# Adding the feed-forward output panels to the residual by ScalarE copies and an accumulating transfer

## What is computed

```python
def swiglu(hn, w_in, w_out):
    gate, up = jnp.split(jnp.einsum('btd,de->bte', hn, w_in), 2, axis=-1)
    return jnp.einsum('btf,fd->btd', jax.nn.silu(gate) * up, w_out)
...
        h = h + swiglu(rmsnorm(h, ffn_norm[i]), ffn_w_in[i], ffn_w_out[i])
        gate = jax.nn.sigmoid(jnp.einsum('btd,de->bte', rmsnorm(h, ple_norm[i]), ple_w_gate[i]))
        h = h + gate * jnp.einsum('btk,kd->btd', p[i], ple_w_proj[i])
    return rmsnorm(h, final_norm)
```

## Time and profile before

| | us |
|---|---|
| median of 3 runs (1648.51 to 1648.92) | 1648.61 |
| the profiled execution's own time | 1648.48 |
| span of its instructions | 1646.7 |
| TensorE busy | 1628.0 |
| VectorE busy | 1224.7 |
| ScalarE busy | 853.0 |

### The profile page before, as it was taken

The page is one execution under the profiler, slowest core; times in us unless marked ns, Lnnn a source line. Parts: engine busy times, 40 slices in busy tenths (PEclk is TensorE's granted clock), DMA queues, the critical chain, the costliest instruction groups (busy, mean ns, idle before and its releaser), DMA issues.

```text
span 1646.7 us, 21708 instructions
## 1 busy us (share of the span) xinstructions
PE 1628.0 (99%) x8508; PEld 1340.5 (81%) x8508; DVE 1224.7 (74%) x1168; ACT 853.0 (52%) x880; POOL 58.6 (4%) x83
## 2 busy tenths in 40 slices
PE   9999999999999999999998999999999999999997
PEld 7888888888888888888887888888888888887886
DVE  5544475566787999765588988988888888888654
ACT  5444454443567655765464545454555544554543
POOL 7000000000010000000000000000000000000001
PEclk9999999999999999999999999999999999999999
DMA  8666655766575655545565546456457366365741
GB/s 277 179 181 189 185 161 167 230 220 215 155 256 166 180 178 180 167 132 181 176 227 205 184 174 243 165 204 229 146 212 254 121 235 238 119 237 215 289 153 51
DMA packets 156776, 316.00 MB, mean 192 GB/s; under 512 B 7360, under 2 KB 7360, under 8 KB 155808
## 3 DMA queue, kind: packets, MB, share of 16 engines
q1 hardware_dynamic: 155088, 304.12, 56.7%
q0 software_dynamic: 1616, 10.87, 1.8%
HBM read 310.77 MB, written 4.19 MB: 191 GB/s over the span
## 4 chain that ended last, share of the span: by engine, by line
PE 97%; DVE 1%; issue 1%; ACT 1%; DMA 0%; POOLq 0%; POOL 0%; DVEq 0%; SPq 0%; ACTq 0%
PE acc L732 15%; PE acc L734 15%; PE acc L733 15%; PE acc L1031 9%; PE acc L1033 9%; PE acc L1032 9%; PE aux L1031 7%; PE aux L1033 7%; PE aux L1032 7%; PE aux L748 1%; PE aux L918 1%; DVE d_lo L2136 1%; PE aux L760 1%; PE acc L1059 0%; PE aux L812 0%
## 5 line engine op out<-in xcount | busy, mean ns | idle before, releaser
L2136 DVE TENSOR_TENSOR d_lo<-d_raw,d_hi 128x2048 fp32r<-128x2048 f32 x181 | 414.1, 2289 | 120.9 <-ACT d_hi L1492 88.8
L1668 DVE TENSOR_TENSOR w_lo<-w_raw,w_hi 128x1024 fp32r<-128x1024 f32 x276 | 335.9, 1224 | 207.6 <-ACT w_hi L1191 207.0
L1191 ACT CAST w_hi<-w_raw 128x1024 fp32r<-128x1024 f32 x276 | 289.5, 1050 | 341.5 <-PE acc L734 312.7
L1492 ACT CAST d_hi<-d_raw 128x2048 fp32r<-128x2048 f32 x137 | 262.3, 1915 | 234.4 <-PE acc L1033 128.9
L732 PE MATMUL acc<-w_hi,a_hi 128*128 128x512 f32 x832 | 330.8, 398 | 0.0
L733 PE MATMUL acc<-w_lo,a_hi 128*128 128x512 f32 x832 | 324.6, 390 | 0.0
L734 PE MATMUL acc<-w_hi,a_lo 128*128 128x512 f32 x832 | 324.6, 390 | 0.0
L734 PEld LDWEIGHTS acc<-w_hi,a_lo 128*128 128x128 f32 x832 | 156.2, 188 | 33.1
L732 PEld LDWEIGHTS acc<-w_hi,a_hi 128*128 128x128 f32 x832 | 156.3, 188 | 31.9 <-issue 0.3
L733 PEld LDWEIGHTS acc<-w_lo,a_hi 128*128 128x128 f32 x832 | 156.5, 188 | 30.6
L1504 ACT CAST d_hi<-d_raw 128x2048 fp32r<-128x2048 f32 x44 | 84.2, 1913 | 124.0 <-PE aux L1033 66.8
(11 more groups left out here) (312 smaller groups left out, 2218.0 us busy)
## 6 DMA issues: line engine op xcount, KB each, us to landing
d_raw<-in_ffn_w_in SPq DMA_DIRECT2D x88, 1024.0 KB, 7.4
w_raw<-in_w_in SPq DMA_DIRECT2D x112, 512.0 KB, 3.7
w_raw<-in_gla_w_in SPq DMA_DIRECT2D x96, 512.0 KB, 3.9
d_raw<-in_ffn_w_out SPq DMA_DIRECT2D x44, 1024.0 KB, 5.1
w_raw<-in_w_out SPq DMA_DIRECT2D x32, 512.0 KB, 4.7
w_raw<-in_gla_w_out SPq DMA_DIRECT2D x32, 512.0 KB, 3.7
d_raw<-in_ple_w_gate SPq DMA_DIRECT2D x16, 1024.0 KB, 5.1
x_raw<-in_x_cols SPq DMA_DIRECT2D x8, 256.0 KB, 7.0
```

What stands on the lines that cost most here:

```text
L1191: nc.scalar.copy(w_hi[u % RING][:], w_raw[u % RING][:]).then_inc(hi_done, 1)
L1492: nc.scalar.copy(d_hi[e % SPLITS][:], d_raw[slot][:]).then_inc(d_hi_done, 1)
L1668: nc.vector.tensor_tensor(w_lo[u % RING][:], w_raw[u % RING][:], w_hi[u % RING][:], ALU.subtract).then_inc(lo_done, 1)
L2136: nc.vector.tensor_tensor(d_lo[e % SPLITS][:], d_raw[slot][:], d_hi[e % SPLITS][:], ALU.subtract).then_inc(d_lo_done, 1)
```

## The change

VectorE no longer adds o0 to o3 to the residual, in any of the ten steps. ScalarE copies each of the 40 panels (80 banks) into one of two buffers `out_copy`, of 512 KB each, in SBUF that the kernel no longer needs by then, and raises `out_read`. POOL waits for each copied panel and issues an accumulating transfer from the buffer to `h_tok` in SBUF, which raises `out_added`. ScalarE waits for `out_added` of the panel two before, before it fills a buffer again. The adds of fe0 to fe3 stay on VectorE (`add_last`), which now also waits until all 20 transfers of the buffer for even or odd panels have landed. POOL issues `emb_back` and `fin_w` from inside this sequence, behind the transfer of o1 of the last step.

```diff
+    out_copy = [at(f"out_copy{r}", [P, TT, N], F32, (48 + 4 * r) * KB) for r in range(2)]
...  # gpsimd
+            def load_last():
                 pool.wait_ge(d_used, LAST["ft4"] + 1)
                 pool.wait_ge(act_ready, TT * NF)
                 pool.wait_ge(emb_out, 16)
                 pool.dma_start(emb_back[:], emb_dram).then_inc(emb_in, 16)
                 pool.dma_start(fin_w[:], final_norm.partition_broadcast(P)).then_inc(fin_in, 16)
+            for m in range(PO * (NF - 1)):
+                pool.wait_ge(out_read, TT * (m + 1))
+                pool.dma_start(h_tok[:, :, (m % PO) * N:(m % PO + 1) * N], out_copy[m % 2][:],
+                               accum_op=ALU.add).then_inc(out_added[m % 2], 16)
+                if m == PO * (NF - 1) - 3:
+                    load_last()
...  # tensor: turn_h2 and the fe panels
-                pe.wait_ge(out_read, tiles_before + TT * (n + 1))
+                pe.wait_ge(fe_read, TT * (n + 1))
...  # scalar
+            def copy_out(n, e, f, i=0, banks=acc[0:2], first=False):
+                act.wait_ge(d_used, i * E_STEP + (e + 1))
+                if n >= 2 or not first:
+                    act.wait_ge(out_added[n % 2], i * 32 + (32 * (f - 1) + 16 * (n // 2)))
+                for t, b in enumerate(banks):
+                    nc.scalar.copy(out_copy[n % 2][:, t, :], b[:]).then_inc(out_read, 1)
                 silu(1, f - 1, i)
+                if not first:
+                    copy_out(3, before["o3"], f - 1, i)
                 quad_high(at, "g1", f, i)
...
                 quad_high(at, "u1", f, i)
+                copy_out(0, at["o0"], f, i, first=first)
                 sum_high(at, "ft2", f, i)
                 if not last:
                     quad_high(at, "o1", f, i)
                     sum_high(at, "ft3", f, i)
                     quad_high(at, "o2", f, i)
                     silu(0, f, i)
+                    copy_out(1, at["o1"], f, i, first=first)
                     sum_high(at, "ft4", f, i)
                     quad_high(at, "o3", f, i)
+                    copy_out(2, at["o2"], f, i)
                 else:
...
                     quad_high(at, "o3", f, i)
+                    copy_out(1, at["o1"], f, banks=acc[2:4])
...
             high_of(E_FE, ("fe", 0))
+            copy_out(2, LAST["o2"], NF - 1)
             split_act(NF - 1, last_hi, aux[0:2])
+            high_of(E_FE + 1, ("fe", 1))
+            copy_out(3, LAST["o3"], NF - 1, banks=acc[2:4])
...  # vector: add_out leaves all its places in ffn_step and behind fe_low(0) and fe_low(1)
-            def add_out(n, e, i=0, banks=acc[0:2]):
-                dve.wait_ge(d_used, i * E_STEP + (e + 1))
+            def add_last(n):
+                dve.wait_ge(d_used, E_FE + n + 1)
+                dve.wait_ge(out_added[n % 2], 32 * (NF - 1))
                 s = slice(n * N, (n + 1) * N)
-                for t, b in enumerate(banks):
-                    nc.vector.tensor_tensor(h_tok[:, t, s], h_tok[:, t, s], b[:], ALU.add).then_inc(out_read, 1)
+                for t, b in enumerate(panel_banks(n)):
+                    nc.vector.tensor_tensor(h_tok[:, t, s], h_tok[:, t, s], b[:], ALU.add).then_inc(fe_read, 1)
```

More of the change, by code:

```diff
@@ L464, in block_kernel @@
         act_turned, act_hi_done, act_lo_done = (sem(n) for n in ("act_turned", "act_hi_done", "act_lo_done"))
-        out_read, gate_read = sem("out_read"), sem("gate_read")
+        out_read, fe_read, gate_read = sem("out_read"), sem("fe_read"), sem("gate_read")
+        out_added = [sem(f"out_added{r}") for r in range(2)]
         block = ctx.enter_context(nc.Block())
@@ L697, in _ @@
             nc.gpsimd.tensor_tensor(rstd[2][:], ms[:], minus_half[:], ALU.pow).then_inc(rstd_done, 1)
[L699 to L703, removed]
+            def load_last():
+                pool.wait_ge(d_used, LAST["ft4"] + 1)
+                pool.wait_ge(act_ready, TT * NF)
+                pool.wait_ge(emb_out, 16)
+                pool.dma_start(emb_back[:], emb_dram).then_inc(emb_in, 16)
+                pool.dma_start(fin_w[:], final_norm.partition_broadcast(P)).then_inc(fin_in, 16)
+            for m in range(PO * (NF - 1)):
[4 more added lines that the diff above has]
+                    load_last()
             pool.wait_ge(fin_in, 16)
@@ L1152, in _ @@
             for n in range(PO):
-                pe.wait_ge(out_read, tiles_before + TT * (n - 1))
+                if n < 2:
+                    pe.wait_ge(out_read, tiles_before + TT * (n - 1))
+                else:
+                    pe.wait_ge(fe_read, TT * (n - 1))
                 quad(E_FE + n, late_banks(n), last_hi, last_lo, 0, True, BOTH)
@@ L1159, in _ @@
                 if n < 2:
-                    pe.wait_ge(out_read, tiles_before + TT * (n + 3))
+                    pe.wait_ge(fe_read, TT * (n + 3))
                 else:
@@ L1577, in split_act, with ffn_step @@
                     nc.scalar.copy(token_half(dst[:, 0:N // P, :], k), by_half(banks[k][:])).then_inc(act_hi_done, 1)
-            def ffn_step(at, f, i=0, last=False):
+            def copy_out(n, e, f, i=0, banks=acc[0:2], first=False):
[4 more added lines that the diff above has]
+                    nc.scalar.copy(out_copy[n % 2][:, t, :], b[:]).then_inc(out_read, 1)
+            def ffn_step(at, before, f, i=0, first=False, last=False):
                 quad_high(at, "g0", f, i)
@@ L1608, in ffn_step @@
                     quad_high(at, "o3", f, i)
-            ffn_step(STEP, 1)
+                    copy_out(1, at["o1"], f, banks=acc[2:4])
+            ffn_step(STEP, FIRST, 1, first=True)
+            before = {name: e - E_STEP for name, e in STEP.items()}
             with act.Fori(1, NF - 2) as i:
-                ffn_step(STEP, 1, i)
-            ffn_step(LAST, NF - 1, last=True)
+                ffn_step(STEP, before, 1, i)
+            ffn_step(LAST, items(NF - 2), NF - 1, last=True)
             high_of(E_FE, ("fe", 0))
+            copy_out(2, LAST["o2"], NF - 1)
             split_act(NF - 1, last_hi, aux[0:2])
-            for n in range(1, PO):
+            high_of(E_FE + 1, ("fe", 1))
+            copy_out(3, LAST["o3"], NF - 1, banks=acc[2:4])
+            for n in range(2, PO):
                 high_of(E_FE + n, ("fe", n))
@@ L2278, in ffn_step @@
                     combine_first_up()
-                else:
-                    add_out(3, before["o3"], i)
                 quad_low(at, "g1", f, i)
@@ L2292, in ffn_step @@
                 quad_low(at, "u1", f, i)
-                add_out(0, at["o0"], i)
                 quad_low(at, "ft2", f, i)
@@ L2300, in ffn_step @@
                     quad_low(at, "o2", f, i)
-                    add_out(1, at["o1"], i)
                     quad_low(at, "ft4", f, i)
@@ L2304, in ffn_step @@
                     quad_low(at, "o3", f, i)
-                    add_out(2, at["o2"], i)
                     multiply(0, f, i)
@@ L2317, in ffn_step @@
                     quad_low(at, "o3", f)
-                    add_out(1, at["o1"], banks=acc[2:4])
             ffn_step(STEP, FIRST, 1, first=True)
@@ L2330, in _ @@
             fe_low(0)
-            add_out(2, LAST["o2"])
             split_act(NF - 1, last_hi, last_lo, aux[0:2])
             fe_low(1)
-            add_out(3, LAST["o3"], banks=acc[2:4])
             fe_low(2)
             fe_low(3)
-            add_out(0, E_FE, banks=late_banks(0))
+            add_last(0)
             for n in range(PO - 1):
                 low_of(E_PG + n, RAW[("pg", n)][0])
-                add_out(n + 1, E_FE + n + 1, banks=late_banks(n + 1))
+                add_last(n + 1)
                 split_h("h2", n, V_PLE)
```

## The result

The changed kernel takes 1668.93 us in the median of 4 runs (1666.57 to 1670.61), the kernel before 1648.56. The ratio is 1.0122, with a 95% interval from 1.0109 to 1.0135: 20 us slower, where 7.5 were forecast. The profiled execution is the longest of the four, 1670.61 us with a span of 1668.9; what follows explains its 22.2 us of span over the 1646.7 of before.

A forecast was written before the change was run, and what follows sets the result against it. TensorE, busy 99% of the span, was taken to bound the kernel. 1648.5 + 0 (adds) + 0 (copies) + 4.5 (loop) + 3.3 (end) = 1656.3, and 0.1 for the median: 1656 us; range 1648 to 1672.

The forecast's parts named there:

- The wait for `cx`: Last step: TensorE's 2.3 us wait for a VectorE combine stays despite the removed adds; gain 0.
- I take 2.4: Engine time chosen for one accumulating transfer, 2.4 us, nearer the upper end of 1.35 to 2.7.
- A: Time one 512 KB accumulating transfer holds the 16 DMA engines; taken as 2.4 us, range 1.35 to 2.7.
- a room of 3.1 us: Step boundary: g1's tile may land 3.1 us after 1202.32, at 1205.3, before TensorE has to wait.
- the formula: Step boundary: two accumulations ahead make g1 land 2A - 0.45 us later; 4.5 us over nine boundaries.
- two-item leads: Loop: casts of ft4, o3 and g0 come 1.1 us later behind ScalarE's copies, hidden inside these leads.
- The end, 3.3 forecast: Last step: 1.6 us of wait ahead of the first transposes plus 1.7 for the clock, 3.3 us.
- 1529.2 + A: Last step: fe3's tile, landing at 1529.2 before, now lands at 1531.6, giving 1.6 us of wait.
- The second mechanism of the text: Last step: o2's transfer, queued behind 3 MB of loads, lands at 1535; `add_last(0)` wants it at 1534.19; 1 us.
- The hidden case: Rival, no change: each transfer costs near 1.35 us and stays hidden, 1649; chance 0.40 together with ScalarE's 2 us at most.
- The slow adder: Rival: at 4 us a transfer, g1 lands 3.0 to 4.5 us late at nine boundaries, 1704; chance 0.13.
- ScalarE's room of 0.9 us ahead of o1: Loop: the copy of o0 delays o1's subtraction by 1.1 us, leaving 0.9 of 2.0 us of room; hidden.

The follow-up runs named there:

- the copies alone: Changed kernel with ScalarE's 80 copies but no transfers and no waits for them, so o0 to o3 are not added: 1649.00 us, ratio 1.0003.
- The plain transfer: Changed kernel with the 40 transfers overwriting the residual instead of adding to it: 1652.38 us, ratio 1.0025.
- o1 and o2 alone: Changed kernel with only the transfers of o1 and o2 issued (20 of 40), o0 and o3 copied and not added: 1664.74 us, ratio 1.0101.
- only o0 and o3: Changed kernel with only the transfers of o0 and o3 issued (20 of 40), o1 and o2 copied and not added: 1649.12 us, ratio 1.0002.
- four buffers: Changed kernel with four copy buffers, o1 to o3 transferred after the load burst except in the last step, two last loads behind all transfers: 1648.25 us, ratio 0.9997.
- the last loads behind: Changed kernel with the two loads of 3 MB issued behind all 40 transfers, not behind the 38th: 1664.68 us, ratio 1.0095.

## Why the prediction was wrong

**Direction and places: right.** Slower, by two things, and both are where the text had them: nine waits of TensorE at g1, because the engines serve two accumulations before its load is through, and one ahead of the first transposes, because fe3's tile comes late beside what POOL issues. The removed adds and the added copies were put at 0 and are 0 (the copies alone, 1.0003). The wait for `cx` was to stay and stayed. The sum was wrong: 7.8 us against 22.1 in the profiled execution. The range held the measured time, the terms did not hold theirs.

**The step that failed is "I take 2.4" for A.** It measured 2.8. The price of a wait at g1 is what is left of a room of 3.1 us, so a small error of A is a large one of the wait. With A = 2.8 and the rest of the text's own working, g1 would land 2 x 2.8 - 0.45 = 5.15 us later, which is 0.6 to 2.1 us late, about 1.3 on the mean and 12 for nine. Measured: 12.6. In the text 0.5 on the mean and 4.5. The bounds were wrong too: the upper one, both operands read at the rate of a plain move, was 2.7. The plain transfer has A = 1.3, against the 1.35 of the lower bound, so the adding one costs 2.2 times a plain one. The rule of the Trainium skill (Collectives: The Full Stack, section "The bandwidth ceiling: the fold count and why AG ≠ RS ≠ AR"), half the bandwidth for a reducing transfer, agrees with the runs better than my choice did: 2.8 against 1.3.

**Two errors beside it.** The table gives the landing of g1 against TensorE's g1: 15.9 - 7.2 = 8.7 us ahead in the kernel before, 14.9 - 11.4 = 3.5 in the changed one, 5.2 later, as the formula has it with 2.8. But with o1 and o2 alone it is 4.8, so a part of the agreement is luck: the 0.4 of o3's transfer were not in the text. And the copies were not wholly inside "two-item leads": they delay the subtraction of o3, and with it the issue of g1's load, by 1.0 us. Where the engines have time to spare this comes off the room (7.9 us ahead with the copies alone). In the changed kernel the engines are full by then and the formula fits without it; how much it adds there was not tried apart.

**The end, 3.3 forecast.** Of it 1.6 was the wait, and 1.7 the clock behind it, which came. The wait was 4.6. In this execution the clock stayed at 1.00 behind the wait for `cx`, where the earlier trace rows have 0.66, so TensorE came to the transposes some 1.7 us sooner and waited that much longer:

```profile
1520.00:1525.00 5.00, 5.00 (x24) 4.13 (x23) 4.90 (x7) 1.91 (x1) 0.00 (x0) 1.00 0.38 126
```

The other error is fe3's landing, 3.7 us later than before and not 2.4. "1529.2 + A" is not the rule that the runs show: fe3 landed 22.4 us after its issue with the copies alone, 24.6 with the same two accumulations at the end but without o0 and o3, 25.3 with plain transfers and 26.5 here, against 22.8 before. What sets these differences is open. The second mechanism of the text, o2's transfer behind 3 MB, did not bind.

**The clock in the loop, 0 forecast.** Waits of 1 to 1.8 us were said to go without a fall. One of the nine, 1.8 us long, had one (0.69 in its window), eight had none. The runs of the changed kernel are spread over 4.0 us where those of the kernel before in the same comparison span 0.4. Falls of the clock are not shown to be the reason: the mean granted clock of the four runs is 0.993 or 0.994, and 0.001 is 1.7 us.

**The rivals.** The hidden case needed A below 1.8: it is what the plain transfer shows in the loop. The slow adder did not come about. ScalarE's room of 0.9 us ahead of o1 held, at 0.590 us a copy.

## What to carry to other kernels

Moving work from one engine to another that both lie beside TensorE's gives nothing, but its transfer is new work for the DMA engines, and these are not idle at all times because they are idle on the mean (0.48 of the loop). Look for the burst: twenty transfers cost 16 us beside loads with 3 us of room and nothing elsewhere. Where only what exceeds a small room is paid, a small error of the price is a large one of the sum: give the forecast at both ends of the price, and not at a value between. And follow a delay through what it frees: a cast that is 1 us late is hidden from TensorE, but the buffer that it frees is loaded 1 us later.

## What the runs showed of the hardware

An accumulating transfer of 512 KB from SBUF to SBUF holds the 16 DMA engines for 2.8 us, the same transfer without the add for 1.3 us; the first goes in 256 data packets, the second in 128. The queue's reported bytes are equal (31.85 MB in both), so under accumulations a share of 1.11 shows only 236 GB/s, where plain loads show 386. POOL needs 1.20 us to issue an accumulation of 256 rows, 0.72 for the same transfer without the add in 128, and 0.60 for `emb_back`. The same wait of 2.3 us for `cx` in the last step has a fall of the clock behind it in four profiles (the kernel before, only o0 and o3, four buffers, the last loads behind) and none in the other four that have the wait.
